# A sum moved to another PSUM tile, and ScalarE's order inside a slot: a two-layer trunk on one Trainium2 core

## The reference

```python
h = rmsnorm(x, gain)
hq, hf, hi, hg, gq, gk, gv, gr, ga = split_cols(h @ w_in, SPLITS)
# eight heads: 4 HGRN2 heads (key width 128), 4 GLA heads (key width 64), value width 128
o = chunk_gated_linear_attention(q, k, v, log_g)   # exp of cumulated gates, pair products, carried state
o = rmsnorm(o, head_gain) * silu(gate)             # per head: sum of squares over the head's 128 features
m = concat(o over heads) @ w_out
x = x + rmsnorm(m, gain)                           # then a squared-ReLU MLP, then layer 1 (attention, MLP)
```

## Time and profile before

| | |
|---|---|
| median of 3 runs | 1285.98 us (1285.61 to 1287.67) |
| the profiled execution | 1285.61 us |
| its span, first to last instruction | 1283.8 us |
| mean granted TensorE clock | 0.993 of full |
| PE busy | 1243.9 us, 97% |
| DVE busy | 674.6 us, 53% |
| ACT busy | 521.4 us, 41% |
| POOL busy | 104.5 us, 8% |

### The profile page before, as it was taken

One profiled execution on the slowest core, in us unless ns is written; L12 is line 12 of the kernel. 1 busy time (PEld: TensorE's weight loads), 2 busy tenths in 40 slices (PEclk: granted clock), 3 DMA queues, 4 the chain that ended last, 5 costly groups with the idle time before them and its releaser, 6 DMA issues.

```text
span 1283.8 us, 16216 instructions
## 1 busy us (share of the span) xinstructions
PE 1243.9 (97%) x5981; PEld 1007.7 (78%) x5981; DVE 674.6 (53%) x1047; ACT 521.4 (41%) x1003; POOL 104.5 (8%) x110
## 2 busy tenths in 40 slices
PE   5999999998999999999999999999999999999997
PEld 3778888887988888888887886657788888888886
DVE  6466767874663443443446336662654343443444
ACT  4543545544632332323437653332642232332332
POOL 2222122300280000000000000000000000000000
PEclk7999999999999999999999999999999999999999
DMA  4321112124333232223232231100333222223321
GB/s 118 99 83 50 51 50 66 52 67 149 107 112 99 93 104 86 96 97 98 99 99 82 67 72 56 46 1 17 123 107 99 87 100 93 97 98 98 99 82 66
DMA packets 94866, 107.96 MB, mean 84 GB/s; under 512 B 15281, under 2 KB 56338, under 8 KB 94802
## 3 DMA queue, kind: packets, MB, share of 16 engines
q1 hardware_dynamic: 93618, 102.64, 25.8%
q0 software_dynamic: 1184, 4.46, 1.0%
HBM read 104.98 MB, written 2.10 MB: 83 GB/s over the span
## 4 chain that ended last, share of the span: by engine, by line
PE 90%; ACT 4%; DVE 4%; DMA 1%; issue 1%; DVEq 0%; ACTq 0%; SPq 0%
PE bank L1350 25%; PE bank L1351 25%; PE bank L1352 25%; PE pp L1480 2%; PE pp L1723 2%; PE pp L1722 2%; PE po L1740 1%; PE pp L1477 1%; PE pp L1389 1%; PE po L1492 1%; PE po L1495 1%; PE pp L1482 1%; PE pp L1351 0%; PE pp L1352 0%; PE pp L1350 0%
## 5 line engine op out<-in xcount | busy, mean ns | idle before, releaser
L1350 PE MATMUL bank<-h_lo,w_hi 128*128 128x512 f32 (+3 forms) x568 | 220.0, 387 | 7.4 <-DVE h_lo L993 5.8
L1351 PE MATMUL bank<-h_hi,w_lo 128*128 128x512 f32 (+3 forms) x568 | 216.8, 382 | 0.0
L1352 PE MATMUL bank<-h_hi,w_hi 128*128 128x512 f32 (+3 forms) x568 | 216.8, 382 | 0.0
L1350 PEld LDWEIGHTS bank<-h_lo,w_hi 128*128 128x128 f32 (+1 forms) x568 | 106.4, 187 | 33.2 <-issue 11.8
L1350 PE MATMUL bank<-wx,a_hi 128*128 128x512 f32 x320 | 126.0, 394 | 5.2 <-DVE wx L463 5.2
L1214 DVE TENSOR_TENSOR tmp<-sq,bank 128x512 f32<-128x512 f32 x64 | 44.0, 687 | 156.2 <-ACT sq L847 156.2
L1352 PE MATMUL bank<-wx,a_hi 128*128 128x512 f32 x320 | 124.6, 390 | 0.0
L1351 PE MATMUL bank<-wx,a_lo 128*128 128x512 f32 x320 | 124.6, 389 | 0.0
L1352 PEld LDWEIGHTS bank<-h_hi,w_hi 128*128 128x128 f32 (+1 forms) x568 | 106.4, 187 | 21.3 <-issue 0.6
L1351 PEld LDWEIGHTS bank<-h_hi,w_lo 128*128 128x128 f32 (+1 forms) x568 | 106.4, 187 | 20.1 <-issue 0.8
L847 ACT ACTIVATE sq<-bank 128x512 f32<-128x512 f32 x64 | 38.3, 598 | 204.3 <-PE bank L1352 204.3
(11 more groups left out here) (282 smaller groups left out, 2058.7 us busy)
## 6 DMA issues: line engine op xcount, KB each, us to landing
stage<-in_mlp_w SPq DMA_DIRECT2D x128, 512.0 KB, 3.6
stage<-in_ev_w_in SPq DMA_DIRECT2D x28, 512.0 KB, 3.7
stage<-in_ev_w_out SPq DMA_DIRECT2D x8, 512.0 KB, 3.5
stage<-in_od_w_out SPq DMA_DIRECT2D x8, 512.0 KB, 3.6
stage<-in_od_w_in SPq DMA_DIRECT2D x10, 256.0 KB, 2.9
x_tok<-in_x SPq DMA_DIRECT2D x4, 512.0 KB, 5.2
gbc<-in_norm_gains POOLq DMA_DIRECT2D x4, 512.0 KB, 4.2
xr<-in_x POOLq DMA_DIRECT2D x1, 2048.0 KB, 9.4
```

Source lines behind the costliest of these rows:

```text
L1350: nc.tensor.matmul(dst, wh, xl_, start=first, stop=False)
L1351: nc.tensor.matmul(dst, wl, xh, start=False, stop=False)
L1352: return nc.tensor.matmul(dst, wh, xh, start=False, stop=last)
```

## The change

Three edits, all in layer 0's slots:

1. Items. Before, the items that belong to a long tile followed by `w` tiles were moved behind the last of these. Now they stand in the long tile's own slot. By the list this moves items from slot 7 to 5, 14 to 12, 19 to 18, 24 to 23, 30 to 29 and 34 to 33, for ACT and DVE.
2. ACT's order in a slot. Before: tile, `head_norm`, `pump`, items. Now: tile, `pump`, items, `head_norm`.
3. The sum of squares goes to `misc` instead of `po`. It waits for the reader of `misc` before it, and the next `transpose_keys`, `chunk_states` or sum waits for the norm that reads it. The next head's outputs wait only for ACT's copy of `po` (`o_read`), not for the norm (`o_rinv`).

```diff
@@ slots
-        its_at = [[] for _ in todo]
-        for a in range(1, n):
-            i = long_[a]
-            while i + 1 < len(todo) and todo[i + 1][1] is None and (todo[i + 1][0] or "z")[0] == "w":
-                i += 1
-            its_at[i] = items[(a - 1) * len(items) // (n - 1):a * len(items) // (n - 1)]
         for i, (tile, col) in enumerate(todo):
             a = long_.index(i) if i in long_ else None
-            its = its_at[i]
+            its = [] if not a else items[(a - 1) * len(items) // (n - 1):a * len(items) // (n - 1)]
@@ ACT
-                inv_rms(po[:, :], P, 0, o_rinv)
+                inv_rms(misc[:, :], P, 0, o_rinv)
...
                 if tile is not None:
                     evacuate(*tile)
+                    if col is not None:
+                        pump(unit_no[tile])
+                for p, lv in items:
+                    decay(p, lv)
                 for o in SUMS[i]:
                     head_norm(o)
-                if col is not None:
-                    pump(unit_no[tile])
-                for p, lv in items:
-                    decay(p, lv)
                 for o in MIXES[i]:
                     head_high(o)
@@ PE
                     if o >= 1:
-                        pe.wait_ge(o_rinv, o)
+                        pe.wait_ge(o_read, o)
...
             def head_sum(o):
                 pe.wait_ge(o_sq, o + 1)
-                pe.wait_ge(o_read, o + 1)
-                nc.tensor.matmul(po[:, :], ones[:, :], sq[:, 0, :], start=True, stop=True).then_inc(o_sum, 1)
+                pe.wait_ge(*misc_read[-1])
+                misc_read.append((o_rinv, o + 1))
+                nc.tensor.matmul(misc[:, :], ones[:, :], sq[:, 0, :], start=True, stop=True).then_inc(o_sum, 1)
```

## The result

The changed kernel takes 1308.46 us in the median of 4 runs (1307.82 to 1311.37), the kernel before 1286.73 (4 runs, 1285.61 to 1287.67): a ratio of 1.0177, 95% interval 1.0163 to 1.0192. It is 21.7 us slower, where 15.5 was forecast and 1306.5 was the top of the range. The direction and the waits were right. The size was not.

The account below looks back on a forecast made before the run. PE, busy 97% of the span, was taken as the bound, so each new wait shows in full. 1.9 + 0.7 + 2.75 + 6.2 + 2.3 + 1.6 (clock) = 15.45 on 1285.61 gave 1301.1, stated as 1301.2 us; range 1295 to 1306.5.

Parts of the forecast that it names:

- slot 8: Before slot 8's tile, PE waits 1.9 us longer because three items precede ACT's emptying of w0's bank.
- slot 19: The sum of head 0 waits for ACT's copy of the keys, delayed by three items in slot 18: +0.7 us.
- slot 27: chunk_states of pack 2 waits for the norm, now last on ACT behind pump and items: +2.75 us.
- slot 33: transpose_keys of pack 4 waits for the norm, now behind pump and three moved items on ACT: +6.2 us.
- slots 36 to 43: Waits for pack 4's states and head 5's norm, less what the third edit wins at head 7: +2.3 us.
- the clock's term: TensorE's clock falls once, after the wait in slot 33, adding 1.6 us.
- the fall at 705 us: After 2.61 us idle, eight matmuls took 3.46 for 1.87 at half clock: 1.6 us lost, used as price.
- a second fall, in slot 27: Rival: the clock also falls at slot 27's wait of 2.75, 1.6 us more, 1302.7 us; chance 0.25.
- edit 3's gain: Head 7's outputs lose a 1.5 us wait, but a FILL part in slot 43 then waits 0.7: 0.8 won.
- The items of slots 12, 23 and 29: Two to four items move there, covered by later tiles or later use of bank and copy: nothing added.
- the late waits melt: Rival: ACT's and DVE's lead from slot 33 removes slot 39's 3.1 us delay, giving 1298.0 us; chance 0.15.
- no new wait counts: Rival: norms are read and w0's bank freed in time, leaving only a 0.8 us gain, 1284.8; chance 0.04.

Follow-up runs that it names:

- after_busy: The changed kernel with matmuls nobody reads filling PE's waits in slots 8, 27, 33, 37 and 38: 1306.66 us, ratio 1.0148.
- items_misc: The kernel before with items in the long tile's own slot and sums in misc, the norm still first on ACT: 1303.08 us, ratio 1.0121.
- misc_only: The kernel before with only the sums of squares moved to misc, the norm still first on ACT: 1299.47 us, ratio 1.0092.
- misc_order: The kernel before with pump and items ahead of the norm and sums in misc, items not moved between slots: 1302.95 us, ratio 1.0134.
- before_again: The kernel before, unchanged, for a second trace: 1290.76 us against 1286.53 us of the same code in the same batch, ratio 1.0018.
- misc_last: The kernel before with the sums of heads 6 and 7 alone in misc: 1287.28 us, ratio 0.9996.
- shift_24: The kernel before with 24 matmuls ahead of slot 8's tile, moving the work behind by 4.5 us without idle time: 1296.34 us, ratio 1.0074.
- after_shift7: The changed kernel with 7 matmuls ahead of slot 9's tile, moving what follows without removing a wait: 1313.68 us, ratio 1.0215.

## Why the prediction was wrong

**The waits: right.** Each was forecast from a row, and measured by the distances above: slot 8 1.9, measured 1.95; slot 19 0.7, measured 0.7 in `after_busy`; slot 27 2.75, measured 2.77; slot 33 6.2, measured 6.24; slots 36 to 43 2.3, measured 1.80 + 1.69 - 0.49 - 0.71 = 2.3. In sum 13.9 forecast, 13.96 measured, and 0.3 in slot 21 that wasn't forecast. The single edits bear out how they arise: edit 3 alone makes 3.45 of slot 33's wait, edit 2 adds 0.95, edit 1 the remaining 1.8, and only together with edit 2 (`items_misc` has no more than `misc_only`).

The 2.3 of slots 36 to 43 is in part luck. For the kernels with fewer edits the same working gave 0.6 to 1 too much (`misc_only`, `misc_order`, `items_misc`), so it doesn't carry over as it stands; why isn't shown.

One sum has a slip without consequence: 1301.1 and the 0.4 of the median make 1301.5, where the prediction says 1301.2.

**The step that failed** is the clock's term of the sum: "so I count one fall, +1.6. The others go from 0 to one fall each." In the profiled execution there are five falls in the slots, and they cost 11.6. In the median it is about 21.7 - 14.3 = 7.4 more than the kernel before loses to its own. The granted clocks of the timed executions bear this out: at the same mean clock of 0.985 the changed kernel took 1307.82 (one execution) and the kernel before 1292.55 to 1292.97 (three), 15 apart, which is the waits nearly alone. The medians of the clock are 0.984 over 13 executions of the changed kernel and between 0.990 and 0.991 over 80 of the kernel before. Three things were wrong in the term.

First, the price of one. I took it from the fall at 705 us, where the clock was low for 3.4. In slot 33 it was low for 10.2 and cost 2.7 beyond the wait, in slots 18 and 21 for 6.8 and cost 3.2 (the wait of 0.7 inside it) and 3.3.

Second, the number behind waits. The waits of slots 27, 33 and 38 each had one in both traces of the changed kernel, the wait of slot 8 in one of the two. `after_busy` takes the three away by keeping PE busy. In the first trace they are worth 1.5 + 2.7 + 1.6 = 5.8. The rival "a second fall, in slot 27" was right and priced as if it were the only one.

Third, falls where PE doesn't wait at all. The prediction looked for idle times only. That the clock also falls in busy stretches of these slots was there to be asked: the three runs shown spread by 2. `before_again`, `misc_last` and `shift_24` show it in slots without any edit. Why the changed kernel has more of them than the kernel before stays open. The wait of slot 19 isn't the cause of the fall in slot 18, which began first. A shift of the work, as in `shift_24`, is one candidate; the small wait in slot 21 another for the fall there. `after_shift7` should have told and didn't.

**The rest.** That edit 3's gain is 0.8 at best was right (`misc_last` has 0.7 in its timeline, none in its median). The items of slots 12, 23 and 29 cost nothing, as forecast. Those of slot 33 do cost 2.4 when edit 1 stands alone; in the changed kernel the wait of slot 33 covers it, so the sum didn't miss it. Of the rivals, "the late waits melt" and "no new wait counts" didn't happen. The range failed because its upper end took two more falls at 1.6, and no bound from both sides was set for the price of one.

No version beat both kernels: `misc_last` is level with the kernel before.

## What to carry to other kernels

List the users of a PSUM buffer in the order of the engine that writes it, with the reader that each waits for, before moving one more into it: the longer waits of this change could be read off to 0.1 us that way (one of 0.3 was missed), and a buffer shared with a slow reader cost far more than the wait it removed.

A wait on a full TensorE costs more than its length. Here 14.3 of waits came with some 7 of lost clock in the median, so a forecast needs a term for it with its own wide bounds. And a kernel whose runs spread by several us has such falls already: take more than one trace before calling a stretch free of them.

## What the runs showed of the hardware

The granted clock fell in stretches in which PE was busy throughout (112 to 119 us in `before_again`, 0.51), in one trace of a kernel and not in the other. The wait of 2.6 on ACT's L907 near 702 us in the kernel before was followed by a fall, and the same wait (ACT y L901, 2.6, near 729 us) in the changed kernel's first trace wasn't. Low stretches inside the kernels lasted 3.4, 6.8 or 10.2 us.

A full fp32r matmul of 128x128 by 128x512 cost 0.43 between pair products of 64 rows in float32, for 0.23 in a stream of its own kind.

With 6 to 25 matmuls in each of the waits of `after_busy` the clock stayed at 1.00 through them.
